# Two-layer encoder trunk on one core: a fourth unnormalised unit, keys and values in 512-column products, and other places for weight roundings and copies in ScalarE's and VectorE's queues

## The chip, the core and the metric

One NeuronCore of a Trainium2 chip runs the whole program. The metric is the device time of one execution in microseconds (us); lower is better. Beside the runs there is one execution recorded by the hardware profiler.

## What is computed

256 tokens of 1024 features go through two layers. Each layer is a mixer of three branches, a gated feed-forward network and a per-layer input gate:

```
h = rmsnorm(x);  q, k, v, cglu, sc_b, sc_c, sc_h, gates = split(h @ w_in)
y_a = window_attention(q, k, v, sinks, bias) @ w_attn_out     # 16 heads, 4 key/value heads of 64
c   = ca * sigmoid(cb)                       # cglu = [ca, cb], 1024 channels each
y_b = silu(layernorm(causal_dwconv31(c) + b)) @ w_conv_out
y_c = (sc_b * causal_dwconv3(sc_c * sc_h)) @ w_sc_out
x  += (g0*y_a + g1*y_b + g2*y_c) @ w_mix_out                  # g = sigmoid(gates)
x  += (silu(h2 @ w_gate) * (h2 @ w_up)) @ w_down              # h2 = rmsnorm(x), hidden 2816
x  += (p @ w_ple) * sigmoid(rmsnorm(x) @ w_ple_gate)
```

After both layers a final rmsnorm follows. All inputs are float32.

## The kernel before, in words

**Products in three parts.** Every product with a weight is made of three matmuls: high part of the weight by high part of the activation, high by low, low by high. The high part is a rounding to fp32r (ScalarE), the low part the rest (VectorE).

**The weight stream.** All weights come in one order, cut into chunks of sixteen 128x128 blocks (1 MB). SyncE loads chunk n into slot n % 5 of `w_raw` once the chunk five places ahead has been used. ScalarE rounds it to `w_hi` (`round_chunk`, L648, its copy is recorded as L646), VectorE subtracts it into `w_lo` (`low_chunk`, L1022 to L1027, recorded as L1026), and counts `lo_ready`. TensorE waits for `lo_ready` at the first block of each chunk. `after_chunk(c)` on either engine means: convert chunk c + 4 now. Nothing decides at run time: each engine carries out its own list in the order of the code, and the place of `after_chunk` between other steps is the place of that conversion in its queue.

**Strips.** A strip (`strip`, L359) is one 128-column piece of an output, with features on partitions and 256 tokens as moving columns: 8 blocks of contraction by 3 matmuls (L355 to L357). Strip s goes to bank s % 4 of PSUM, and waits until the strip four before it has been read (`bank_read`). Two strips use one chunk. In the later stages `tok_group` (L377, matmuls L393 to L395) works the other way round: tokens on partitions, 512 weight columns as moving ones, two chunks per group of 4 x 12 matmuls.

**Start of a layer.** The first stage (cglu) has 16 strips: 2u is the gate of unit u, 2u + 1 its value. The normalised h isn't ready when it begins. So the strips of units 0 to UNITS - 1 (3 units, strips 0 to 5) are computed from x times the gain (`u_src`), and VectorE multiplies with 1/rms afterwards: `raw_gate` (L1090, recorded L1093) reads the gate strip, ScalarE takes the sigmoid in place (`raw_activate`, L736, counts `gate_done`), and `raw_product` (L1096) waits for it, multiplies again (L1099) and multiplies the value strip into `cv` (L1103). From strip 6 on TensorE uses `h_hi`, `h_lo`: VectorE makes a tile of h (`normalise_tiles`, L1053), ScalarE rounds it (`round_h`, L669), VectorE subtracts (L1030). For later units ScalarE reads the bank itself (`activate`, L709) and VectorE makes one product (L1125).

In the same stretch ScalarE makes products for the 31-tap convolution of four channel tiles (`conv_products`, four at a time in this stage, L646 into `cprod`), which GpSimd adds up (L1511); a ring of four buffers and `pool_step` hold them together. VectorE carries out the taps of two other tiles (L1143, L1148), five per chunk.

**Queries, keys, values.** Twelve strips follow: two of K, two of V, eight of Q. ScalarE copies each out. Then TensorE turns V (four transposes, L468), ScalarE copies it to `v_tok`, and the attention runs inside the sc stage: step j holds weigh_values(j-2) (L503), scores(j) (L479, L481), a strip, and a second strip with `probs_transpose(j-1)` (L492) after its third block. `probs_transpose(t)` waits for `attn_lo` of head pair t - 1, which VectorE makes behind softmax(t + 1). ScalarE does, per step, exponentials(j) and then `copy_probs(j - 1)`.

**End of a layer.** The ple stage has eight short strips (two blocks each), which ScalarE copies out of their banks into `qm`; before the first it rounds a chunk. The ple_gate stage has eight strips of 8 blocks; x is updated tile by tile behind them, and the next layer's strip 0 needs all eight tiles.

## Time and profile before

| | us |
|---|---|
| runs of the kernel before | 1129.14, 1131.5, 1130.98 (median 1130.98) |
| profiled execution | 1129.25 |
| its span, first to last instruction | 1127.4 |
| TensorE busy | 1106.0 (98% of the span) |
| VectorE busy | 814.3 (72%) |
| ScalarE busy | 682.1 (61%) |
| GpSimd busy | 350.0 (31%) |
| mean granted TensorE clock | 0.995 of full speed |

The time of an execution has 1.8 us outside the span. Shares are means over the whole; the matmuls of TensorE overlap each other in the records, so a record's duration is longer than the time from its start to the next one's. In the timeline rows, the first number is the start in us from the span's start, the second the duration.

### The profile page before, as it was taken

The numbers are of one execution on the slowest core, as the hardware profiler recorded it, in microseconds if no ns is written. First come the engines' busy times: TensorE is split into PE (matmuls) and PEld (weight loads), VectorE is DVE, ScalarE is ACT, GpSimd is POOL, SyncE is SP. The second block draws the span as 40 slices with busy tenths as digits, with TensorE's granted clock in tenths as the row PEclk, the third lists the DMA queues.
The fourth block names the chain that finished last, engine by engine and source line by source line (L and its number), as shares of the span: only waits on it lengthen the run. The fifth ranks groups of instructions, "written<-read, shape, count | busy, mean of one in ns | idle before, by whom it ended". The sixth has DMA issues, their size and how long they took to land.

```text
span 1127.4 us, 18108 instructions
## 1 busy us (share of the span) xinstructions
PE 1106.0 (98%) x7202; PEld 1002.1 (89%) x7202; DVE 814.3 (72%) x1209; ACT 682.1 (61%) x1049; POOL 350.0 (31%) x319
## 2 busy tenths in 40 slices
PE   8899999999999999999989999999999999999997
PEld 8899899888898889889989989988888988998997
DVE  7987997898766554555799789878977665545554
ACT  6767875755746443445676788766475554334464
POOL 0787335874001000001129753458530100000011
PEclk9999999999999999999999999999999999999999
DMA  9564334555555545555545534355555455555541
GB/s 362 197 237 156 120 144 168 201 192 187 196 187 181 185 157 200 184 189 177 186 150 176 180 133 151 120 191 203 197 196 187 176 178 187 177 186 183 185 150 38
DMA packets 29347, 201.42 MB, mean 179 GB/s; under 512 B 3520, under 2 KB 3712, under 8 KB 5840
## 3 DMA queue, kind: packets, MB, share of 16 engines
q1 hardware_dynamic: 27648, 195.38, 49.4%
q0 software_dynamic: 1088, 4.74, 1.2%
q8 instruction: 57, 0.93, 0.3%
q10 hardware_dynamic: 528, 0.15, 0.1%
q14 instruction: 26, 0.21, 0.0%
HBM read 199.19 MB, written 3.69 MB: 180 GB/s over the span
## 4 chain that ended last, share of the span: by engine, by line
PE 90%; DVE 4%; ACT 3%; issue 1%; DMA 1%; SPq 0%; DVEq 0%
PE bank L393 15%; PE bank L395 15%; PE bank L394 15%; PE bank L355 14%; PE bank L356 14%; PE bank L357 14%; ACT w_hi L646 1%; DMA w_raw<-in_wstream 1%; DVE w_lo L1026 1%; PE bank L503 1%; PE bank L571 1%; PE bank L492 1%; PE bank L479 0%; PE bank L535 0%; ACT probs L772 0%
## 5 line engine op out<-in xcount | busy, mean ns | idle before, releaser
L1026 DVE TENSOR_TENSOR w_lo<-w_raw,w_hi 128x2048 fp32r<-128x2048 f32 x183 | 427.8, 2342 | 169.9 <-ACT w_hi L646 169.8
L646 ACT ACTIVATE w_hi<-w_raw 128x2048 fp32r<-128x2048 f32 (+1 forms) x185 | 350.7, 1899 | 116.3 <-DMA w_raw<-in_wstream 116.3
L1511 POOL TENSOR_TENSOR pacc<-pacc,cprod 128x256 f32<-128x256 f32 x224 | 253.1, 1130 | 124.8 <-ACT cprod L646 98.7
L355 PE MATMUL bank<-h_hi,w_hi 128*128 128x256 f32 x864 | 249.3, 289 | 6.1 <-issue 6.1
L356 PE MATMUL bank<-h_lo,w_hi 128*128 128x256 f32 x864 | 245.6, 284 | 0.0
L357 PE MATMUL bank<-h_hi,w_lo 128*128 128x256 f32 x864 | 245.5, 284 | 0.0
L393 PE MATMUL bank<-w_hi,h_hi 128*128 128x512 f32 x544 | 214.3, 394 | 0.0
L395 PE MATMUL bank<-w_hi,h_lo 128*128 128x512 f32 x544 | 212.1, 390 | 0.0
L394 PE MATMUL bank<-w_lo,h_hi 128*128 128x512 f32 x544 | 211.8, 389 | 0.0
L355 PE MATMUL bank<-act_hi,w_hi 128*128 128x256 f32 x608 | 173.8, 286 | 4.0 <-ACT qm L646 1.1
L355 PEld LDWEIGHTS bank<-h_hi,w_hi 128*128 128x128 f32 x864 | 166.8, 193 | 10.7 <-issue 10.7
L356 PE MATMUL bank<-act_lo,w_hi 128*128 128x256 f32 x608 | 172.0, 283 | 0.0
L357 PE MATMUL bank<-act_hi,w_lo 128*128 128x256 f32 x608 | 172.0, 283 | 0.0
L356 PEld LDWEIGHTS bank<-h_lo,w_hi 128*128 128x128 f32 x864 | 167.0, 193 | 0.0
L357 PEld LDWEIGHTS bank<-h_hi,w_lo 128*128 128x128 f32 x864 | 166.8, 193 | 0.0
L1474 POOL TENSOR_TENSOR sqsum<-cprod 128x256 f32<-128x256 f32 x6 | 4.4, 738 | 466.8 <-ACT cprod L662 466.8
L646 ACT ACTIVATE cprod<-cv,prms 128x256 f32<-128x256 f32 x248 | 113.0, 504 | 48.6 <-POOL pacc L1511 48.6
L355 PEld LDWEIGHTS bank<-act_hi,w_hi 128*128 128x128 f32 x608 | 116.5, 192 | 6.4 <-issue 1.9
L395 PEld LDWEIGHTS bank<-w_hi,h_lo 128*128 128x128 f32 x544 | 102.1, 188 | 21.8
L394 PEld LDWEIGHTS bank<-w_lo,h_hi 128*128 128x128 f32 x544 | 102.2, 188 | 20.5
L393 PEld LDWEIGHTS bank<-w_hi,h_hi 128*128 128x128 f32 x544 | 102.2, 188 | 20.4
L356 PEld LDWEIGHTS bank<-act_lo,w_hi 128*128 128x128 f32 x608 | 116.6, 192 | 0.3
(168 smaller groups left out, 1377.0 us busy)
## 6 DMA issues: line engine op xcount, KB each, us to landing
w_raw<-in_wstream SPq DMA_DIRECT2D x183, 1024.0 KB, 4.9
rel_bias_rows<-rel_bias_by_distance POOLq DMA_DIRECT2D x1, 2560.0 KB, 15.5
bias<-rel_bias_rows POOLq DMA_DIRECT2D x1, 1536.0 KB, 8.6
xs<-in_x SPq DMA_DIRECT2D x2, 512.0 KB, 5.6
w_raw<-in_wstream SPq DMA_DIRECT2D x2, 512.0 KB, 6.5
out_y<-xs SPq DMA_DIRECT2D x4, 256.0 KB, 2.4
zacc<-in_p POOLq DMA_DIRECT2D x2, 256.0 KB, 2.9
prms<-in_prm SPq DMA_DIRECT2D x1, 328.0 KB, 9.8
```

The source lines that it names most:

```text
L355: nc.tensor.matmul(o, wh, hi, start=first, stop=False, skip_group_check=True)
L356: nc.tensor.matmul(o, wh, lo, start=False, stop=False, skip_group_check=True)
L357: return nc.tensor.matmul(o, wl, hi, start=False, stop=last, skip_group_check=True)
L393: nc.tensor.matmul(o, hi[:, t0 + kt, rows], wh, start=kt == 0, stop=False, skip_group_check=True)
L394: nc.tensor.matmul(o, hi[:, t0 + kt, rows], wl, start=False, stop=False, skip_group_check=True)
L395: mm = nc.tensor.matmul(o, lo[:, t0 + kt, rows], wh, start=False, stop=kt == DT - 1, skip_group_check=True)
L492: mm = nc.tensor.transpose(psum[6 + e][:, c * P:(c + 1) * P], probs[:, t % 2, e, c * P:(c + 1) * P], idt[:, :])
L503: mm = nc.tensor.matmul(psum[6][rows, b * P:SEQ], v_tok[:, b, v], probs_t[:, e, b * SEQ:SEQ + b * P], start=b == 0, stop=b == 1, skip_grou ...
L571: mm = nc.tensor.transpose(psum[6 + n % 2][:, e * SEQ + b * P:e * SEQ + (b + 1) * P], prod[:, b, e * P:(e + 1) * P], idt[:, :])
L646: return nc.scalar.activation(o, i, ACT.Identity, **kw)
L1026: nc.vector.tensor_tensor(w_lo[:, slot, :], w_raw[:, slot, :], f32(w_hi[:, slot, :]), ALU.subtract).then_inc(lo_ready, 1)
L1511: nc.gpsimd.tensor_tensor(o, a, cprod[:, n % PROD_RING, :], ALU.add).then_inc(pool_step, 1)
```

## The change

It has five parts. (1) UNITS goes from 3 to 4, so strips 6 and 7 too use x times gain; the order of units, normalised tiles and the conversion of chunk 3 in both queues is another. (2) K and V are one `tok_group` of two chunks, tokens on partitions, columns 0 to 255 K and 256 to 511 V; now K is turned by four transposes, inside the second Q strip, and V is copied out directly. (3) In the sc stage ScalarE does `copy_probs(0)` before exponentials(1). (4) At the ple stage the conversion of one chunk goes behind the fourth strip's copy on ScalarE. (5) At the ple_gate stage ScalarE's rounding of the next layer's chunk 1 goes behind all eight tiles.

```diff
-UNITS = 3
+UNITS = 4
...
-                for s in range(2 * KT + QT):
-                    strip(L, S0["qkv"] + s, BPC * C0["qkv"] + DT * s, h_src, DT)
-
-
-                def v_transpose():
+                def turn_k():
+
                     for b in range(TB):
+                        pe.wait_ge(bank_read[2 + b], L * USES + S0["qkv"] // BANKS + 2)
+                        pe.wait_ge(bank_read[b], L * USES + S0["qkv"] // BANKS + 2)
                         for t in range(KT):
-                            if b == 0:
-                                wait_read(pe, L, S0["qkv"] + KT + t, (S0["qkv"] + KT + t) % BANKS)
-                            mm = nc.tensor.transpose(psum[6][:, b * KT * P + t * P:b * KT * P + (t + 1) * P],
-                                                     vv[:, t, b * P:(b + 1) * P], idt[:, :])
-                    mm.then_inc(vt_done, 1)
+                            mm = nc.tensor.transpose(psum[6][:, t * SEQ + b * P:t * SEQ + (b + 1) * P],
+                                                     k_tok[:, b, t * P:(t + 1) * P], idt[:, :])
+                    mm.then_inc(kt_done, 1)
+
+                tok_group(L, S0["qkv"], C0["qkv"], h_src, 0, L * USES + S0["qkv"] // BANKS + 1)
+                for s in range(2 * KT, 2 * KT + QT):
+                    strip(L, S0["qkv"] + s, BPC * C0["qkv"] + DT * s, h_src, DT, amid=turn_k if s == 2 * KT + 1 else None)
...
-                v_transpose()
+                pe.wait_ge(kk_ready, L + 1)
...
-                round_h(L * 3)
+                raw_activate(1, 2, ACT.Sigmoid)
                 round_chunk(L, AHEAD - 1)
+                round_h(L * 3, range(0, DT // 2))
+                raw_activate(2, 4, ACT.Sigmoid)
+                round_h(L * 3, range(DT // 2, DT))
                 for t in range(DT):
                     if t >= UNITS:
                         activate(t, 2 * t, ACT.Sigmoid, 2 * (t - 2) + 1)
-                    elif t > 0:
+                    elif t > 2:
                         raw_activate(t, 2 * t, ACT.Sigmoid)
...
+                def kv_out():
+
+                    s, use = S0["qkv"], L * USES + S0["qkv"] // BANKS + 1
+                    for b in range(TB):
+                        wait_strip(act, L, s + 2 + b)
+                        act.wait_ge(bank_read[2 + b], use)
+                        copy(k_tok[:, b, :], psum[b][:, 0:KT * P]).then_inc(bank_read[2 + b], 1)
+                        copy(v_tok[:, b, :], psum[b][:, KT * P:2 * KT * P]).then_inc(bank_read[b], 1)
+
+                def k_out():
+
+                    act.wait_ge(kt_done, L + 1)
+                    copy(kk[:, :, :].rearrange("p a b -> p (a b)"), psum[6][:, :]).then_inc(kk_ready, 1)
+
                 for s in range(2 * KT + QT):
-                    g = S0["qkv"] + s
-                    wait_strip(act, L, g)
-                    dst = kk[:, s, :] if s < KT else vv[:, s - KT, :] if s < 2 * KT else qm[:, s - 2 * KT, :]
-                    copy(dst, psum[g % BANKS][:, 0:SEQ], scale=1.0 if s < 2 * KT else HEAD_DIM ** -0.5
-                         ).then_inc(bank_read[g % BANKS], 1)
+                    if s == 2 * KT - 1:
+                        kv_out()
+                    if s >= 2 * KT:
+                        g = S0["qkv"] + s
+                        wait_strip(act, L, g)
+                        copy(qm[:, s - 2 * KT, :], psum[g % BANKS][:, 0:SEQ], scale=HEAD_DIM ** -0.5
+                             ).then_inc(bank_read[g % BANKS], 1)
+                    if s == 2 * KT + 2:
+                        k_out()
                     if s % 2:
                         after_chunk(C0["qkv"] + s // 2 - 1)
                         conv_products(before_qkv + QKV_PRODUCTS * (s // 2 + 1))
                 nc.scalar.activation(unused[:, :], eps[:, :], ACT.Exp)
-                act.wait_ge(vt_done, L + 1)
-                copy(v_tok[:, :, :], psum[6][:, 0:TB * KT * P].rearrange("p (b f) -> p b f", b=TB)).then_inc(vtok_ready, 1)
...
                     if j == 0:
                         exponentials(0)
                     after_chunk(C0["sc"] + j - 1)
+                    if j == 1:
+                        copy_probs(0)
                     if 0 < j < QT:
                         exponentials(j)
-                    if 0 <= j - 1 < QT:
+                    if 1 <= j - 1 < QT:
                         copy_probs(j - 1)
...
-                for c in range(done, DT * FB // BPC - 1):
-                    after_chunk(C0["down_b"] + c)
                 for t in range(DT):
                     s = S0["ple"] + t
                     wait_strip(act, L, s)
                     copy(qm[:, t, :], psum[s % BANKS][:, 0:SEQ]).then_inc(bank_read[s % BANKS], 1)
+                    if t == 3:
+                        for c in range(done, DT * FB // BPC - 1):
+                            after_chunk(C0["down_b"] + c)
...
-                    if t == 5:
-                        after_chunk(C0["ple_gate"] + 1)
 
                 for t in (DT - 2, DT - 1):
                     act.wait_ge(ple_added, L * DT + t + 1)
                     next_high(t)
                     square(L * 3 + 3, t)
-                after_chunk(C0["ple_gate"] + 2)
+                for c in (1, 2):
+                    after_chunk(C0["ple_gate"] + c)
...
+                def raw_unit(u):
+                    raw_gate(u, 2 * u)
+                    raw_product(cv[:, u, CPAD:], u, 2 * u + 1, u)
+
                 inverse(L * 3)
-                raw_gate(0, 0)
+                raw_unit(0)
+                raw_unit(1)
+                low_chunk(L, AHEAD - 1)
                 normalise_tiles(L * 3, L, G_MIX, range(0, DT // 2))
-                raw_product(cv[:, 0, CPAD:], 0, 1, 0)
+                raw_unit(2)
                 normalise_tiles(L * 3, L, G_MIX, range(DT // 2, DT))
-                raw_gate(1, 2)
-                low_chunk(L, AHEAD - 1)
-                raw_product(cv[:, 1, CPAD:], 1, 3, 1)
-                raw_gate(2, 4)
-                raw_product(cv[:, 2, CPAD:], 2, 5, 2)
+                raw_unit(3)
...
-        strips += [cols(k, t) for t in range(KT)] + [cols(v, t) for t in range(KT)]
+        strips.append(np.concatenate([side(m, 0, KT).reshape(DT, KT, P, P) for m in (k, v)], axis=1))
```

ScalarE's queue at the start of the first layer, before (`w_hi<-w_raw` are chunks 3, 4, 5; the sigmoids, L736, are those of units 0, 1 and 2, `cprod` the convolution products):

```order
L736 ACTIVATE gated<-gated 128x256 [waits bank_read0]
L646 ACTIVATE h_hi<-hf 128x256 [waits hf_ready] x8
L646 ACTIVATE w_hi<-w_raw 128x2048 [waits raw_loaded3]
L736 ACTIVATE gated<-gated 128x256 [waits bank_read2]
L646 ACTIVATE w_hi<-w_raw 128x2048 [waits raw_loaded4]
L646 ACTIVATE cprod<-cv,prms 128x256 [waits bank_read1]
L646 ACTIVATE cprod<-cv,prms 128x256 x3
L736 ACTIVATE gated<-gated 128x256 [waits bank_read0]
L646 ACTIVATE w_hi<-w_raw 128x2048 [waits raw_loaded0]
```

The same place in the changed kernel (line numbers are its own; L734 are the sigmoids of units 0 to 3):

```order
L734 ACTIVATE gated<-gated 128x256 [waits bank_read0]
L734 ACTIVATE gated<-gated 128x256 [waits bank_read2]
L644 ACTIVATE w_hi<-w_raw 128x2048 [waits raw_loaded3]
L644 ACTIVATE h_hi<-hf 128x256 [waits hf_ready] x4
L734 ACTIVATE gated<-gated 128x256 [waits bank_read0]
L644 ACTIVATE h_hi<-hf 128x256 [waits hf_ready] x4
L644 ACTIVATE w_hi<-w_raw 128x2048 [waits raw_loaded4]
L644 ACTIVATE cprod<-cv,prms 128x256 [waits bank_read1]
L644 ACTIVATE cprod<-cv,prms 128x256 x3
L644 ACTIVATE w_hi<-w_raw 128x2048 [waits raw_loaded0]
L644 ACTIVATE cprod<-cv,prms 128x256 [waits pool_step] x4
L734 ACTIVATE gated<-gated 128x256 [waits bank_read2]
```

Units 0 and 1 and chunk 3 moved ahead of the normalised tiles; the last row is the sigmoid of unit 3, behind chunks 4 and 5 and eight products.

VectorE's queue at the end of the normalised tiles, in the changed kernel (L1111, L1117, L1121 are unit 3, the first `w_lo` row is chunk 4, the next chunk 5):

```order
L1048 TENSOR_TENSOR h_lo<-hf,h_hi 128x256 [waits hhi_ready] x2
L1111 TENSOR_TENSOR gated<-bank,rstd 128x256 [waits strip_done]
L1117 TENSOR_TENSOR gated<-gated,rstd 128x256 [waits gate_done]
L1121 TENSOR_TENSOR cv<-bank,gated 128x256 [waits strip_done,gate_scaled]
L1044 TENSOR_TENSOR w_lo<-w_raw,w_hi 128x2048 [waits hi_ready]
L1163 TENSOR_SCALAR bank<-cv,prms 128x256 [waits bank_read3]
L1168 SCALAR_TENSOR_TENSOR bank<-cv,prms,bank 128x256 [waits conv_step] x4
L1044 TENSOR_TENSOR w_lo<-w_raw,w_hi 128x2048 [waits hi_ready]
```

Before, three units (of them unit 0 amid the tiles) and chunk 3 stood ahead of chunk 4; now unit 3 is the last step ahead of it.

## Rows read from the trace of the kernel before

**Rows 1.** Waits of TensorE: line, waited for, us in total, times, longest.
```profile
PE bank L355 <- issue: 6.1, 2, 3.7
PE bank L503 <- ACT probs_t L646: 3.3, 2, 1.7
...
PE bank L355 <- ACT qm L646: 1.1, 2, 0.6
```

**Rows 2.** Timeline of TensorE around strips 6 to 8, first layer: start, duration.
```profile
29.00 0.28 PE L357 MATMUL bank<-act_hi,w_lo 128*128 128x256 f32 x1
32.97 0.50 PE L355 MATMUL bank<-h_hi,w_hi 128*128 128x256 f32 x1 [3.69 <-issue]
...
37.42 0.28 PE L355 MATMUL bank<-h_hi,w_hi 128*128 128x256 f32 x1
...
40.30 0.28 PE L355 MATMUL bank<-h_hi,w_hi 128*128 128x256 f32 x1
```

**Rows 3.** Stretch table: us, busy of PE, PEld, DVE, ACT, POOL; clock, DMA.
```profile
32.97:36.38 3.41, 3.41 (x16) 3.41 (x17) 2.66 (x6) 3.41 (x7) 2.19 (x3) 0.51 0.56 232
```

**Rows 4.** Timeline of VectorE, start of the first layer.
```profile
21.73 0.42 DVE L1093 TENSOR_TENSOR gated<-bank,rstd 128x256 f32<-128x256 f32 x1
22.07 0.87 DVE L1053 SCALAR_TENSOR_TENSOR hf<-xs,prms,rstd 128x256 f32<-128x256 f32 x2
...
24.49 0.42 DVE L1099 TENSOR_TENSOR gated<-gated,rstd 128x256 f32<-128x256 f32 x1
24.95 0.42 DVE L1103 TENSOR_TENSOR cv<-bank,gated 128x256 f32<-128x256 f32 x1
...
30.58 2.29 DVE L1026 TENSOR_TENSOR w_lo<-w_raw,w_hi 128x2048 fp32r<-128x2048 f32 x1 [1.04 <-ACT w_hi L646]
...
35.97 2.37 DVE L1026 TENSOR_TENSOR w_lo<-w_raw,w_hi 128x2048 fp32r<-128x2048 f32 x1
```

**Rows 5.** Timeline of ScalarE in the same stretch.
```profile
22.18 0.42 ACT L736 ACTIVATE gated<-gated 128x256 f32<-128x256 f32 x1 [2.82 <-DVE gated L1093]
...
28.65 1.90 ACT L646 ACTIVATE w_hi<-w_raw 128x2048 fp32r<-128x2048 f32 x1
...
30.76 1.89 ACT L646 ACTIVATE w_hi<-w_raw 128x2048 fp32r<-128x2048 f32 x1
32.56 1.78 ACT L646 ACTIVATE cprod<-cv,prms 128x256 f32<-128x256 f32 x4
34.25 0.40 ACT L736 ACTIVATE gated<-gated 128x256 f32<-128x256 f32 x1
34.55 1.90 ACT L646 ACTIVATE w_hi<-w_raw 128x2048 fp32r<-128x2048 f32 x1
```

**Rows 6.** Timeline of VectorE, second layer's start.
```profile
568.27 5.04 DVE L1026 TENSOR_TENSOR w_lo<-w_raw,w_hi 128x2048 fp32r<-128x2048 f32 x2
...
575.01 0.42 DVE L1093 TENSOR_TENSOR gated<-bank,rstd 128x256 f32<-128x256 f32 x1
```

**Rows 7.** Timeline of TensorE, second layer: first matmuls of strips 6 and 8.
```profile
586.26 0.55 PE L355 MATMUL bank<-h_hi,w_hi 128*128 128x256 f32 x1 [2.42 <-issue]
...
593.46 0.28 PE L355 MATMUL bank<-h_hi,w_hi 128*128 128x256 f32 x1
```

**Rows 8.** Timeline of VectorE, later in the cglu stage.
```profile
50.70 2.30 DVE L1026 TENSOR_TENSOR w_lo<-w_raw,w_hi 128x2048 fp32r<-128x2048 f32 x1
52.92 2.04 DVE L1148 SCALAR_TENSOR_TENSOR bank<-cv,prms,bank 128x256 f32<-128x256 f32 x5
...
55.22 2.44 DVE L1026 TENSOR_TENSOR w_lo<-w_raw,w_hi 128x2048 fp32r<-128x2048 f32 x1
```

**Rows 9.** Timeline of TensorE in a stage with 512 moving columns.
```profile
200.03 0.39 PE L394 MATMUL bank<-w_lo,act_hi 128*128 128x512 f32 x1
200.26 0.39 PE L395 MATMUL bank<-w_hi,act_lo 128*128 128x512 f32 x1
200.48 0.39 PE L393 MATMUL bank<-w_hi,act_hi 128*128 128x512 f32 x1
```

**Rows 10.** Timeline of VectorE in step 2 of the sc stage.
```profile
119.55 0.41 DVE L1030 TENSOR_TENSOR act_lo<-bank,act_hi 128x256 fp32r<-128x256 f32 x1
```

**Rows 11.** Timeline of TensorE in the same step.
```profile
120.11 0.85 PE L492 MATMUL bank<-idt,probs 128*128 128x128 f32 x6 [0.16 <-DVE act_lo L1030]
```

More of the change, by code:

```diff
@@ L172, in build @@
         kk = sb("kk", [P, KT, SEQ])
-        vv = part
+        k_tok = part
         v_tok = sb("v_tok", [P, TB, KT * P])
@@ L239, in build @@
         hlo_ready = sem("hlo_ready")
-        vt_done = sem("vt_done")
-        vtok_ready = sem("vtok_ready")
+        kt_done = sem("kt_done")
+        kk_ready = sem("kk_ready")
         s_done = sem("s_done")
@@ L488, in probs_transpose @@
                             pe.wait_ge(attn_lo, L * QT + t)
-                        if e == 0 and t == 0:
-                            pe.wait_ge(vtok_ready, L + 1)
                         for c in range(3):
@@ L498, in weigh_values @@
                     pe.wait_ge(pt_copied, L * 2 * QT + 2 * t + 2)
-                    pe.wait_ge(vtok_ready, L + 1)
                     for b in range(TB):
@@ L667, in root, with round_h @@
                 nc.scalar.activation(rstd[:, :], psum[4][:, 0:SEQ], ACT.Sqrt, bias=eps[:, :]).then_inc(std_ready, 1)
-            def round_h(q):
-                for t in range(DT):
+            def round_h(q, tiles):
+                for t in tiles:
                     act.wait_ge(hf_ready, q // 3 * DT + t + 1)
```

## The prediction

> **What bounds the kernel now.** I read the page first: TensorE is busy in 98% of the span, so only two things can shorten the kernel, fewer TensorE cycles or fewer of its waits. Then the waits of TensorE [rows 1]. The reader is to see that they are few: two of 3.7 and 2.4 us put down to "issue", two before weigh_values (3.3 us in all), two of some 0.6 us on ScalarE's `qm` copies. Then the timelines around each, to see what really ended it. The first "issue" wait lies before strip 6: the matmul before it starts at 29.00 and strip 6 at 32.97 [rows 2]. It isn't h that is late but chunk 3: VectorE's subtraction runs from 30.58 to 32.87 [rows 4] and TensorE starts 0.10 later. Its rounding starts at 28.65 [rows 5], behind all eight tiles of h. The second layer repeats this. A stall costs more than its length: in the 3.4 us behind it the granted clock is 0.51, that is the lower level, 1.2 GHz [rows 3]. At full clock a strip takes 40.30 - 37.42 = 2.88 us [rows 2], so two take 5.76; strips 6 and 7 took 7.33 in the first layer [rows 2] and 7.20 in the second [rows 7], 1.57 and 1.44 us more.
>
> **Part 1, the fourth unit, layer 1.** I follow the changed queues with the durations of before; all times are on the clock of the old trace, where everything up to the first raw gate (21.73) stays. Unit 0: gate at 21.73, its sigmoid 0.45 later [rows 4, 5], the multiplication with 1/rms 0.45 after that (sigmoid 0.42, hand-over 0.03), the product 0.46 later (24.49 to 24.95), the next gate 0.34 later (21.73 to 22.07): 1.70 in all [rows 4]. Unit 1's gate is at 23.43, its sigmoid at 23.88, the rounding of chunk 3 0.30 later (34.25 to 34.55 [rows 5]) at 24.18. Rounding and subtraction took 28.65 to 32.87, 4.22 [rows 4, 5], so chunk 3 is ready at 28.40, ahead of strip 6 (29.12): the old stall goes, and strip 8 could start at 29.12 + 5.76 = 34.88.
>
> It can't, because of chunk 4. The first tile of h starts at about 28.35; four tiles later comes unit 2's gate, 2.42 after the first tile (22.07 to 24.49 [rows 4]), 30.77; its product 0.45 + 0.45 + 0.46 later, 32.13 (0.1 more for ScalarE's last tile in between: 32.2). From such a product to the next rounding, across the last four tiles, it took 24.95 to 28.65, 3.70 [rows 4, 5]: chunk 4's rounding starts at 35.9. ScalarE then has, **ahead of unit 3's sigmoid**, chunk 4 (1.80, from 30.76 to 32.56), four products (1.69, to 34.25), chunk 5 (1.80) and four more products (1.69): 6.98 [rows 5]. The sigmoid starts at 42.9. VectorE stands at unit 3 all this time, and chunk 4's subtraction stands behind unit 3 on VectorE. From sigmoid to the end of the subtraction it took 34.25 to 35.97 + 2.37 = 38.34, 4.09 [rows 4, 5]; with 0.10 to TensorE, strip 8 starts at 47.1 instead of 40.30: **+6.8**. TensorE idles some 12 us, and resumes on the lower clock: another 1.57, since the old loss lies within the old 40.30. Behind the wait on VectorE queue chunk 4's and 5's subtractions and the early taps; ScalarE isn't held. They catch up: a round of subtraction, five taps and a product takes 4.52 (50.70 to 55.22 [rows 8]) against 5.76 per chunk on TensorE, so I cost them at nothing; uncovered, each lost round would cost up to 5.8 - 4.5, with the sign against the kernel.
>
> **Layer 2.** The same chain is 25.4 long from the first raw gate (47.1 - 21.73). That gate was at 575.01, behind a pair of subtractions of 5.04 [rows 6]. Part 5 puts both roundings behind the last tile; the two then take 1.8 + 1.9 and the last subtraction 2.3 where the pair took 5.04: +1.0. The last tile itself comes sooner, since no 1.9 us rounding is ahead of it. Bounds of the net: 0 and 1.9; I take 0.5, nearer the small end. So strip 8 starts at 575.01 + 0.5 + 25.4 = 600.9 instead of 593.46 [rows 7]: **+7.4**, and the clock again, 1.44. Part 5's gain at strip 0 is swallowed here: strip 8 hangs on the queues, not on when strip 0 began.
>
> **Part 2, K and V.** Removed: 4 strips, 96 matmuls of 256 columns, one per 2.88 / 24 = 0.120 us, 11.52. Added: 48 of 512 columns, one per 0.227 (200.03 to 200.48 is two [rows 9]), 10.90. The recorded durations (0.28 and 0.39) would say 26.9 against 18.7, but they overlap. **-0.6 per layer, -1.2 in all.** Transposes and copies are as many as before; V's copy leaves the stretch before exponentials(0), K's goes between Q copies, hidden under strips of 2.88.
> The Trainium skill, page "TensorE: Matmul & The Clock Gate", section "Back-to-back issue gap", gives about 131 ns for a sustained 512-column matmul; by that the group would take 6.3 us and the change save 5.2 a layer, 9 us more in all than I count. The trace contradicts it for these fp32r products (0.227), and the trace decides.
>
> **Part 3, copy_probs(0).** TensorE's 1.65 us wait before weigh_values(0) goes, two times [rows 1]. What is late next: 14 matmuls and the scores later comes `probs_transpose(1)`, which waits for `attn_lo` of pair 0. VectorE reaches it at 119.55 to 119.96 [rows 10], and TensorE already waited there (it starts at 120.11 [rows 11]). VectorE's row of steps to it doesn't start at weigh_values, so TensorE merely waits 1.7 us later. Bounds: -3.3 (all kept) and +2.9 (nothing kept, and a wait of about 2 us that drops the clock as the 2.4 us one did). I take **0**, since the row shows the next wait in place.
>
> **Part 4, ple copies.** The 1.1 us before strip 4's bank go [rows 1]: the four copies are done before the rounding. The rounding ends before strip 4's own copy is needed by ple_gate. **-1.1**; bounds -1.5 and 0.
>
> **Sum.** 6.8 + 1.6 + 7.4 + 1.4 - 1.2 + 0 - 1.1 = +14.9. From the profiled execution's own 1129.25 that is 1144.1. The median of the runs before lies 1.7 above that execution, which I can't carry over in full, since three runs spread by 2.4; I take 0.7 of it: **1144.8**.
>
> **Rivals.**
> A, the other side: *nothing takes the old stall's place.* It needs chunk 4 at TensorE by 34.9, 12 us earlier than above, so either unit 3's sigmoid isn't awaited by VectorE's next subtraction, or ScalarE reaches it before chunk 4. For it: the old stall does go (chunk 3 is ready 0.7 early). Against: the order of both queues. It decides from the point where the subtraction ends before 40.2; between that and 34.9 the change is faster. Time: -6.1 of waits [rows 1], -3.0 of clock, -1.2, -1.1 (and up to -3.3 for part 3): 1129.25 - 11.4 = 1117.9, down to 1114.6. Chance 0.06.
> The same page of the Trainium skill (section "Architectural detail: the array is 16× 32×32, not 1× 128×128") says that ScalarE's and VectorE's queues are strictly first in, first out. By that rule the subtraction of chunk 4 can't pass unit 3, and A is out; rows 4 and 5 show no step that passed another.
> B: *as forecast, but with a tail.* The late convolution products, VectorE's catch-up, or a clock fall in the attention stage add to it: +3 for a clock fall in both layers, up to 1.3 for each of some rounds not caught up. For: TensorE's new wait in part 3 (about 2 us) lies between waits of 1.65 without and 2.4 with a fall. Time: 1147 to 1151. Chance 0.17.
> C: *the sigmoid comes sooner than I count*, because ScalarE's products overlap or unit 3's steps take 0.42 where the old ones were stretched. Each layer up to 1.5 less, and part 3 kept: 1138 to 1141. Chance 0.10.
> D: *the change isn't what it says*, unit 3 is still normalised in time by another path, or the parts cancel. Then within 0.2% of before, 1128.7 to 1133.2. Chance 0.02.
>
> **How the numbers follow.** The forecast has 0.65; the time is its own. The range takes in most of B and C: 1139.5 to 1149.5, which leaves out A, D and the far ends of B and C, some 0.15. A measurement of this kernel tells from no change about 0.2%, 2.3 us. Slower by more: forecast, B and C, 0.92. Same: D, 0.02. Faster: A, 0.06.
>
> **What would show it.** In the changed trace: no wait before strip 6 in either layer; one of about 12 us before strip 8, put down to "issue" or VectorE's `w_lo`, with the clock near 0.5 in the 3.4 us behind it; VectorE idle for 6 to 7 us before the second multiplication of unit 3; ScalarE's fourth in-place sigmoid behind two roundings and eight products. 48 matmuls of 512 columns 0.227 apart in 10.9 us. No wait before weigh_values(0), but one of 1.5 to 2 us before `probs_transpose(1)`. No `qm` wait at the ple stage. I am wrong if strip 8 follows strip 7 without a gap, if the 512-column pitch of that group is much below 0.227, or if the clock stays low long after the stall.

## The result, and the profile after

| | before | changed |
|---|---|---|
| median of 4 runs | 1130.17 (1129.14 to 1131.5) | 1144.32 (1143.9 to 1145.2) |
| profiled execution, its span | 1129.25, 1127.4 | 1143.97, 1141.8 |

The ratio is 1.0123, 95% interval 1.0111 to 1.0135: 14 us slower, against 1144.8 forecast. The page's part 1 of the changed kernel has nearly the same busy times on every engine as before, in a longer span (the 96 matmuls fewer are the K/V groups):

```profile
PE 1104.6 (97%) x7106; PEld 997.7 (87%) x7106; DVE 813.8 (71%) x1213; ACT 682.3 (60%) x1049; POOL 350.2 (31%) x319
```

TensorE's waits in the changed kernel (line, waited for, us in total, times, longest):

```profile
PE bank L355 <- issue: 22.6, 2, 11.7
PE bank L491 <- DVE act_lo L1048: 3.7, 2, 1.9
```

The "issue" waits have grown from 6.1 to 22.6 [rows 1]. Those before weigh_values and at the ple stage are gone from the list, and one before `probs_transpose(1)` is new. The timeline of TensorE shows that the large ones lie before strip 8 of each layer:

```profile
34.52 0.28 PE L357 MATMUL bank<-act_hi,w_lo 128*128 128x256 f32 x1
46.46 0.55 PE L355 MATMUL bank<-h_hi,w_hi 128*128 128x256 f32 x1 [11.66 <-issue]
...
607.22 0.55 PE L355 MATMUL bank<-h_hi,w_hi 128*128 128x256 f32 x1 [10.95 <-issue]
```

Strips 6 and 7 now follow strip 5 without a gap, where strip 6 had waited [rows 2]. The "gaps" below are from the start of the last matmul before a wait to the start of the next one: 11.94 and 11.23 us here. Matmuls that don't wait start 0.12 us apart, so that much of a gap is no wait. "Issue" names nobody, so the next step is ScalarE's timeline in the gap:

```profile
35.56 0.42 ACT L644 ACTIVATE h_hi<-hf 128x256 fp32r<-128x256 f32 x1 [0.32 <-DVE hf L1071]
35.88 1.89 ACT L644 ACTIVATE w_hi<-w_raw 128x2048 fp32r<-128x2048 f32 x1
37.68 1.78 ACT L644 ACTIVATE cprod<-cv,prms 128x256 f32<-128x256 f32 x4
39.37 1.89 ACT L644 ACTIVATE w_hi<-w_raw 128x2048 fp32r<-128x2048 f32 x1
41.17 1.69 ACT L644 ACTIVATE cprod<-cv,prms 128x256 f32<-128x256 f32 x4
42.76 0.40 ACT L734 ACTIVATE gated<-gated 128x256 f32<-128x256 f32 x1
```

and VectorE's:

```profile
36.35 0.42 DVE L1111 TENSOR_TENSOR gated<-bank,rstd 128x256 f32<-128x256 f32 x1
43.19 0.42 DVE L1117 TENSOR_TENSOR gated<-gated,rstd 128x256 f32<-128x256 f32 x1 [6.43 <-ACT gated L734]
43.65 0.42 DVE L1121 TENSOR_TENSOR cv<-bank,gated 128x256 f32<-128x256 f32 x1
43.99 2.36 DVE L1044 TENSOR_TENSOR w_lo<-w_raw,w_hi 128x2048 fp32r<-128x2048 f32 x1
```

Read together: chunk 4 is rounded by 37.8, but its low part starts at 43.99, because VectorE stands for 6.43 us at unit 3, whose sigmoid comes after two roundings and eight convolution products. TensorE starts 0.11 after the subtraction ends. The stretch table (us, busy of PE, PEld, DVE, ACT, POOL; granted clock, DMA) shows the price behind the gap:

```profile
46.46:51.20 4.74, 4.74 (x22) 4.74 (x23) 4.60 (x7) 0.51 (x1) 4.31 (x4) 0.50 0.00 2
...
607.22:611.50 4.28, 4.28 (x20) 4.28 (x21) 4.14 (x6) 0.51 (x1) 3.85 (x4) 0.50 0.00 0
```

The granted clock is 0.50 there, the lower level, 1.2 GHz. It stays so until 52.02 in the first layer and 611.81 in the second, 5.6 and 4.6 us of matmuls, where it was 3.4 before [rows 3].

The new wait in the attention and K/V's group, on TensorE and VectorE:

```profile
125.98 0.28 PE L357 MATMUL bank<-h_hi,w_lo 128*128 128x256 f32 x1
128.12 0.41 PE L491 MATMUL bank<-idt,probs 128*128 128x128 f32 x2 [1.87 <-DVE act_lo L1048]
```

```profile
127.56 0.42 DVE L1048 TENSOR_TENSOR act_lo<-bank,act_hi 128x256 fp32r<-128x256 f32 x1
```

```profile
72.00 0.40 PE L393 MATMUL bank<-w_hi,h_hi 128*128 128x512 f32 x1
...
82.91 0.28 PE L355 MATMUL bank<-h_hi,w_hi 128*128 128x256 f32 x1
```

A ledger of how late the changed kernel is at one place after another, each against the same place in the kernel before: strip 10 of layer 1 +8.66 (54.72 against 46.06), scores(0) +8.02, probs_transpose(1) +8.0 (128.12 against 120.11, [rows 11]), ple's mean square +7.2, strip 10 of layer 2 +15.84 (615.06 against 599.22), scores(0) +15.2, last instruction +14.4. So 8.66 comes in at each layer's start, 0.64 goes at each K/V group and 0.8 at each ple stage, and nothing changes in the attention.

### The profile page after: what moved, and what is told of

The parts are those of the page before. It is cut to its first block, busy times and chain, and to the rows that moved or that the text cites. A ratio compares the mean times of both kernels' runs of the same rounds, so it can differ in the third digit from the quotient of the medians.

```text
span 1141.8 us, 17902 instructions
## 1 busy us (share of the span) xinstructions
PE 1104.6 (97%) x7106; PEld 997.7 (87%) x7106; DVE 813.8 (71%) x1213; ACT 682.3 (60%) x1049; POOL 350.2 (31%) x319
## 4 chain that ended last, share of the span: by engine, by line
PE 92%; DVE 3%; issue 2%; ACT 2%; DMA 0%; DVEq 0%
PE bank L393 15%; PE bank L395 15%; PE bank L394 15%; PE bank L355 14%; PE bank L356 14%; PE bank L357 14%; PE bank L501 1%; DVE w_lo L1044 1%; PE bank L569 1%; PE bank L491 1%; ACT w_hi L644 1%; DMA gain<-in_gain 0%; PE bank L480 0%; PE bank L533 0%; ACT act_hi L644 0%
## 5 line engine op out<-in xcount | busy, mean ns | idle before, releaser
L355 PE MATMUL bank<-h_hi,w_hi 128*128 128x256 f32 x768 | 223.0, 290 | 22.6 <-issue 22.6
L393 PE MATMUL bank<-w_hi,h_hi 128*128 128x512 f32 x576 | 226.7, 394 | 0.0
L395 PE MATMUL bank<-w_hi,h_lo 128*128 128x512 f32 x576 | 224.5, 390 | 0.0
L394 PE MATMUL bank<-w_lo,h_hi 128*128 128x512 f32 x576 | 224.3, 389 | 0.0
L356 PE MATMUL bank<-h_lo,w_hi 128*128 128x256 f32 x768 | 219.1, 285 | 0.0
L357 PE MATMUL bank<-h_hi,w_lo 128*128 128x256 f32 x768 | 218.9, 285 | 0.0
L356 PE MATMUL bank<-act_lo,w_hi 128*128 128x256 f32 x640 | 181.0, 283 | 0.0
L355 PEld LDWEIGHTS bank<-h_hi,w_hi 128*128 128x128 f32 x768 | 149.1, 194 | 27.3 <-issue 27.2
L356 PEld LDWEIGHTS bank<-h_lo,w_hi 128*128 128x128 f32 x768 | 149.3, 194 | 0.1
L357 PEld LDWEIGHTS bank<-h_hi,w_lo 128*128 128x128 f32 x768 | 149.1, 194 | 0.0
```

Of the source, the lines that this page charges most:

```text
L355: nc.tensor.matmul(o, wh, hi, start=first, stop=False, skip_group_check=True)
L356: nc.tensor.matmul(o, wh, lo, start=False, stop=False, skip_group_check=True)
L357: return nc.tensor.matmul(o, wl, hi, start=False, stop=last, skip_group_check=True)
L393: nc.tensor.matmul(o, hi[:, t0 + kt, rows], wh, start=kt == 0, stop=False, skip_group_check=True)
L394: nc.tensor.matmul(o, hi[:, t0 + kt, rows], wl, start=False, stop=False, skip_group_check=True)
L395: mm = nc.tensor.matmul(o, lo[:, t0 + kt, rows], wh, start=False, stop=kt == DT - 1, skip_group_check=True)
```

## Experiments

**1. Unit 3's sigmoid alone, moved.** On ScalarE only, against the changed kernel:

```diff
                 round_h(L * 3, range(DT // 2, DT))
+                raw_activate(3, 6, ACT.Sigmoid)
                 for t in range(DT):
...
-                    elif t > 2:
-                        raw_activate(t, 2 * t, ACT.Sigmoid)
```

> The changed kernel with one move: ScalarE takes unit 3's sigmoid right behind the last tile of h, ahead of chunk 4's rounding, the eight products and chunk 5's. Queue theory (chunk 4's subtraction waits behind unit 3, which waits for ScalarE): VectorE's gate of unit 3 ends at 36.8, the sigmoid follows, chunk 4 is rounded 37.1 to 39.0 and subtracted by 41.4, so strip 8 starts at 41.4 instead of 46.5, in the second layer also about 5 earlier; less clock loss as well: 1134 us, 10 less than the changed kernel, 4 more than the kernel before. Rival 1 (chunk 4 is late because its own rounding or its load is late, unit 3 only stands beside it): strip 8 still at 46.5, 1144. Rival 2 (fourth unit's extra VectorE work costs the time): no change either, within 1 us of 1144.

Measured 1136.5, ratio 1.0052 (1.0037 to 1.0067). Strip 8 starts at 41.43 instead of 46.46, and what ends its wait is now chunk 4's rounding, which stands behind the eighth tile of h:

```profile
36.79 0.42 ACT L734 ACTIVATE gated<-gated 128x256 f32<-128x256 f32 x1 [0.83 <-DVE gated L1110]
37.11 1.89 ACT L644 ACTIVATE w_hi<-w_raw 128x2048 fp32r<-128x2048 f32 x1
39.04 2.29 DVE L1043 TENSOR_TENSOR w_lo<-w_raw,w_hi 128x2048 fp32r<-128x2048 f32 x1 [0.92 <-ACT w_hi L644]
41.43 0.55 PE L355 MATMUL bank<-h_hi,w_hi 128*128 128x256 f32 x1 [6.39 <-issue]
```

TensorE's waits:

```profile
PE bank L355 <- issue: 12.3, 2, 6.4
PE bank L491 <- DVE act_lo L1047: 3.7, 2, 1.9
PE bank L355 <- ACT v_tok L644: 2.3, 2, 1.5
```

One instruction's place in ScalarE's queue is worth 8 of the 14 us. The gaps before strip 8 are still 6.67 and 6.21. 1134 was expected. The third row has 2.3 us of what is missing: with the start 5 us earlier ScalarE is held by GpSimd's ring of four products, and V's copy comes late. In the recorded execution a fall of the clock in the attention took another 1.5 (the last section has its row).

**2. Part 1 alone.** The kernel before with the four units and the order of both queues around them, nothing else:

```diff
-UNITS = 3
+UNITS = 4
...
-                round_h(L * 3)
+                raw_activate(1, 2, ACT.Sigmoid)
                 round_chunk(L, AHEAD - 1)
+                round_h(L * 3, range(0, DT // 2))
+                raw_activate(2, 4, ACT.Sigmoid)
+                round_h(L * 3, range(DT // 2, DT))
...
```

> The kernel before with part 1 alone (fourth unit, new order at a layer's start); K and V as four strips, the copies and roundings elsewhere as before. Queue theory: part 1 is worth +16.5 (8.7 in the first layer; in the second 7.2 to 8.7, since part 5's later roundings are missing), so 1146 to 1147, slower than the changed kernel by 2 to 3. Rival (the loss comes from the K/V group or from an interplay of parts): 1135 or less.

Measured 1146.03, ratio 1.0144 (1.0125 to 1.0164). Its profile has gaps of 11.93 and 10.41 before strip 8. All of the slowdown is part 1's: 8 us of it the place of unit 3's sigmoid, by experiment 1.

**3. All but part 1.** The changed kernel with part 1 undone, so with parts 2 to 5:

```diff
-UNITS = 4
+UNITS = 3
```

> The changed kernel with part 1 undone: three units in the old order, parts 2 to 5 as changed. Queue theory: -1.2 for K and V, -1.4 for the ple stage, 0 for copy_probs, and up to -0.5 at the second layer's start: 1127.3, with both old waits of 3.9 and 2.7 us before strip 6 back and the wait before probs_transpose(1) at about 2.1 us. Rival (part 3 does pay by itself when the layer's start doesn't disturb it): 1124.

Measured 1128.43 (10 runs), ratio 0.9979 (0.9967 to 0.9991). The start's stall is back before strip 6, with gaps of 4.22 and 3.55 where they had been 3.97 and 2.70. The 0.85 more in layer 2 isn't what part 5 costs. Counted from the mean square of the ple stage, strip 0 starts 0.38 sooner (28.17 instead of 28.55) and strip 6 0.31 later (47.38 instead of 47.07): the price is 0.3, and the rest of the longer gap is strips 0 to 5 being done sooner. After the shorter of the two gaps no fall of the clock followed in the recorded execution:

```profile
586.20:590.00 3.80, 3.80 (x34) 3.80 (x33) 3.08 (x5) 3.80 (x7) 2.38 (x4) 1.00 0.13 52
33.20:38.30 5.10, 5.10 (x25) 5.10 (x26) 4.35 (x6) 4.92 (x10) 3.49 (x4) 0.53 0.33 135
```

**4. Part 3 alone.** The kernel before, and on ScalarE:

```diff
+                    if j == 1:
+                        copy_probs(0)
                     if 0 < j < QT:
                         exponentials(j)
-                    if 0 <= j - 1 < QT:
+                    if 1 <= j - 1 < QT:
                         copy_probs(j - 1)
```

> The kernel before with part 3 alone: copy_probs(0) ahead of exponentials(1). Theory that the wait only moves: the 1.8 us before weigh_values(0) go in both layers, and the wait before probs_transpose(1) grows from 0.3 to 2.1: 1130.2, the same within 0.2%, perhaps 0.3 worse, since V's copy still stands ahead of exponentials(0). Rival (VectorE's chain starts from scores(2) and moves with TensorE): -3.3, 1126.9.

Measured 1130.47, ratio 0.9997 (0.9987 to 1.0007). The wait before weigh_values(0) goes and one before `probs_transpose(1)` comes (3.8 us in two, where the old had been 3.3): the same time.

**5. Part 2 alone.** The kernel before, and on TensorE (with its copies and the weights' order as in the change):

```diff
-                for s in range(2 * KT + QT):
+                tok_group(L, S0["qkv"], C0["qkv"], h_src, 0, L * USES + S0["qkv"] // BANKS + 1)
+                for s in range(2 * KT, 2 * KT + QT):
...
```

> The kernel before with part 2 alone: K and V as one group of 48 matmuls with 512 columns. Pitch theory (0.120 us per 256-column matmul, 0.227 per 512-column one, whatever the recorded durations say): -0.6 per layer, 1129.0 if 1130.2 is the kernel before, ratio 0.9989. V's copy also leaves ScalarE's way to exponentials(0), so the waits in the attention stage may shrink by up to 0.5 each. Rival (recorded durations 0.28 and 0.39 are the cost): -8 per layer, 1114.

Measured 1128.78 (11 runs; before 1130.92), ratio 0.9981 (0.9972 to 0.9989), 2.1 us less. The pitch (the time from one matmul's start to the next one's) accounts for 1.2, at the edge of the interval, and the recorded execution has just that: from strip 6 to scores(0) it is 0.70 shorter in the first layer and 0.51 in the second. Where the other 0.9 comes from isn't shown. Part of it may be the clock: of the 20 runs of the kernel before, 8 had a mean granted clock of 0.991, of these 11 none had less than 0.993.

**6. Chunks 3, 4 and 5 early.** On top of experiment 1, ScalarE rounds all three before the first tile of h, VectorE makes 3 and 4 before the tiles and 5 before unit 3:

```diff
-                round_chunk(L, AHEAD - 1)
+                for n in (3, 4, 5):
+                    round_chunk(L, n)
                 round_h(L * 3, range(0, DT // 2))
...
-                        after_chunk(t - 1)
+                        if t > 2:
+                            after_chunk(t - 1)
...
```

> The kernel of e1 with chunks 4 and 5 rounded right behind chunk 3 on ScalarE, chunk 4 subtracted right behind chunk 3 and chunk 5 ahead of unit 3 on VectorE. Queue theory: chunk 4 is ready at 30.7, four us ahead of strip 8 (34.7); strip 8 loses at most 1.6 us to the last tiles of h (tile 7 at 38.7 where 37.2 is wanted), and the clock doesn't fall. But the convolution products start at 38.9 against strip 8 at 34.7, so GpSimd's ring holds ScalarE: I expect a wait for ScalarE before strip 12 (1 to 3 us) and before the first Q strip (3 to 7 us). Together 1122 to 1127, still 10 under e1. Rival (the late data of chunk 4 isn't the last thing, h is): strip 8 starts after 38.

Measured 1135.49, ratio 1.0038 (1.0025 to 1.0052), 8 us or more above what was expected. The wait before strip 8 is gone, another stands before strip 12:

```profile
PE bank L355 <- ACT gated L707: 7.2, 2, 3.7
PE bank L491 <- DVE act_lo L1049: 3.7, 2, 1.9
```

ScalarE's timeline shows why: it stands at the products, and strip 8's gate is read only then.

```profile
47.49 1.29 ACT L644 ACTIVATE cprod<-cv,prms 128x256 f32<-128x256 f32 x3
50.67 0.51 ACT L644 ACTIVATE cprod<-cv,prms 128x256 f32<-128x256 f32 x1 [1.89 <-POOL pacc L1534]
51.09 0.36 ACT L707 ACTIVATE gated<-bank 128x256 f32<-128x256 f32 x1
```

**7. The same with fewer products in this stage**, none at the first step of K and V, and the late ones over more chunks:

```diff
-CGLU_PRODUCTS, QKV_PRODUCTS, SC_PRODUCTS = 4, 4, 3
-LATE_CHUNKS = 8
+CGLU_PRODUCTS, QKV_PRODUCTS, SC_PRODUCTS = 3, 4, 3
+LATE_CHUNKS = 10
...
```

> The kernel of e6 with the convolution products spread otherwise: three instead of four per chunk in the cglu stage, none at the first step of the qkv stage, the rest in ten instead of eight later steps. If GpSimd's ring is what holds ScalarE in e6, its waits before strip 12 and before the Q strips go or fall under 1 us and nothing is late at the conv mean: 1118 to 1120. Rival (ScalarE's own work, not the ring, is late): as e6, or slower where the products come later.

Measured 1135.26, ratio 1.0036 (1.0022 to 1.005), again far above what was expected. TensorE's waits for ScalarE's gates and copies went, and two others came in each layer: gaps of 2.5 and 2.7 before strip 12, for a low part that VectorE makes behind ten taps, and one of 3.56 at the convolution's mean. Ten chunks are too many: in experiment 12, with nine, the second is gone.

```profile
PE bank L545 <- POOL sqsum L1547: 6.3, 2, 3.2
```

**8. Attention: the low part first.** Experiment 3 with the low part of attn(j - 2) ahead of softmax(j) on VectorE:

```diff
+                    if 0 <= j - 2 < QT:
+                        low_attn(j - 2)
                     if j < QT:
                         softmax(j)
...
-                    if 0 <= j - 2 < QT:
-                        low_attn(j - 2)
```

> The kernel of e3 (parts 2 to 5 without part 1) with VectorE's subtraction for attn_lo ahead of softmax instead of behind it. If the wait before probs_transpose(1) is VectorE's order alone, it falls from 2.1 to about 0.6 us in both layers, -3.0 together: ratio 0.995 to before, 3 us under e3. Rival (that wait hangs on scale_probs(1) or on ScalarE's rounding): within 1 us of e3.

Measured 1127.08, ratio 0.9964 (0.9955 to 0.9974), the lowest median here, though its interval overlaps those of experiments 3 and 11. It is 1.35 less than experiment 3, and not the 3 that were expected. Of the gap of 2.15 some 0.7 is left, and a new one of 1.6 per layer stands before weigh_values(1):

```profile
PE bank L501 <- ACT probs_t L644: 2.7, 2, 1.3
```

**9. Early chunks, spread out.** As 7, but chunks 6 to 11 one step earlier on both engines, and other numbers of products. On VectorE:

```diff
-                    if t > 2:
-                        after_chunk(t - 1)
-                    taps(min(CGLU_TAPS * t, CGLU_DONE) if t < DT - 1 else CGLU_DONE)
+                    if 1 < t < 5:
+                        after_chunk(t)
+                    if t > 0:
+                        taps(min(CGLU_TAPS * t, CGLU_DONE) if t < DT - 1 else CGLU_DONE)
+                    if t > 4:
+                        after_chunk(t)
```

> The change with unit 3's sigmoid first, chunks 3, 4 and 5 rounded in a row before the first tiles, and now every later cglu chunk (6 to 11) one step earlier on both engines instead of from the third step on, so that VectorE no longer makes ten taps ahead of chunk 6's low part; GpSimd's products 3 a step in the cglu part, none at the first qkv step, 5 at the others, and the rest over nine chunks instead of ten. The run before this one had lost the start's stall but had got waits of 2.5 and 2.7 us before strip 12 and of 3.6 us at the convolution's mean, each in both layers, and 3.4 us of half clock behind each. Theory (those were places where work that had been put off fell due, and no new law): all four go, 1135.3 - 5.1 - 7.1 - some 4 of clock = 1119, 1117 to 1122. Rival (ScalarE and VectorE are full between strips 8 and 16, so whatever is moved from before strip 8 comes back as a wait there or in the qkv part): a wait of 2 us or more of TensorE for a chunk's low part, ScalarE's copies or the gates, and 1127 to 1136.

Measured 1136.51, ratio 1.005 (1.0035 to 1.0065). The rival was nearer: TensorE still waits for the gates, and the longest wait is now in the attention, which neither had named. The expectation also counted the lower clock behind the waits before strip 12. In experiment 7's profile it had followed only those at the mean (0.58 from 266.50 to 270.00); behind strip 12 the clock was 1.00 (50.35 to 54.00, 606.22 to 610.00).

```profile
PE bank L491 <- DVE act_lo L1051: 5.7, 2, 2.8
PE bank L355 <- ACT gated L707: 3.6, 2, 2.0
PE bank L501 <- ACT probs_t L644: 3.1, 2, 1.6
```

**10. The same with both moves in the attention**, that of 8 and on ScalarE:

```diff
-                    if j == 1:
-                        copy_probs(0)
+                    if j in (1, 2):
+                        copy_probs(j - 1)
...
-                    if 1 <= j - 1 < QT:
+                    if 2 <= j - 1 < QT:
```

> The kernel of the run before plus the attention's order: the low part of attn(t-2) ahead of softmax(t) on VectorE, and copy_probs(1) ahead of exponentials(2) on ScalarE as copy_probs(0) is. Theory (the two waits of 2.15 us before the values of block 2 go, the one of 1.6 before weigh_values(1) that took their place does not come): 3 to 4 us less than that run, plus what a clock fall behind them had cost. Rival (with copy_probs(1) first, the exponentials of 2 come late and transposing them waits instead): the same as that run within 1 us.

Measured 1135.3, ratio 1.0037 (1.0023 to 1.0052): 1.2 less in the median, not 3 to 4, and the intervals overlap. The recorded executions took the same, 1135.39 here and 1135.34 in experiment 9, so this is the rival's outcome. TensorE's waits for `probs_t` are now eight, 6.8 us, those for `act_lo` 2.8: 9.6 together, where they had been 3.1 and 5.7, 8.8 together.

**11. Experiment 3 with both moves in the attention.**

> The change without part 1, with both moves in the attention. The run with the low part alone ahead had 1127.08 and waits of 1.62 us before weigh_values(1) in each layer, from copy_probs(1) behind exponentials(2). Theory: with copy_probs(1) ahead those go to the 0.5 us or so of a step's own chain, 1.1 us less a layer: 1124.9, ratio 0.9945. Rival: exponentials(2), late by copy_probs(1)'s 1 us, let transpose(2) or its values wait by as much, and the time stays at 1127.

Measured 1127.37, ratio 0.9971 (0.9959 to 0.9983), the same as experiment 8. The two waits of 1.3 became six:

```profile
PE bank L355 <- issue: 7.4, 2, 4.1
PE bank L501 <- ACT probs_t L644: 2.8, 6, 0.6
```

**12. Experiment 7 with two edits**, the low part first as in 8 and:

```diff
-LATE_CHUNKS = 10
+LATE_CHUNKS = 9
```

> The kernel that had chunks 3 to 5 rounded early and three products a step (1135.26), with two edits: its late products spread over nine chunks instead of ten, and the low part of attn(t-2) ahead of softmax(t) on VectorE. In its profile the wait of 3.56 us at the convolution's mean stood in each layer with 3.4 us of half clock behind it, and the values of block 2 waited 1.8 and 2.1 us. Theory (each of these waits is its own and nothing but PE's time stands behind it): 7.1 and some 3.4 of clock go at the mean, 2 to 3 in the attention, so 1122, ratio 0.992, the fastest of all. Rival (VectorE and ScalarE are full and each wait removed comes back in the next place, as it did in the three kernels with early chunks so far): 1130 or more, with a new wait of over 2 us named in the profile.

Measured 1128.46 (1125.59 to 1132.55, 10 runs), ratio 0.9985 (0.9971 to 1.0). The waits at the mean went and nothing took their place: 6.8 less than experiment 7. That is about half of what was expected, and neither theory's number. In the attention the waits for `act_lo` fell from 3.4 to 0.4 and one of 2.7 for `probs_t` came. What is left:

```profile
PE bank L355 <- DVE w_lo L1045: 5.6, 3, 2.4
PE bank L501 <- ACT probs_t L644: 2.7, 2, 1.3
```

So four units, with everything around them put in order, come to the time of three (experiment 3), and not below it. The fair comparison is experiment 8, which has three units and the same order in the attention: 0.9964 (0.9955 to 0.9974) against 0.9985 (0.9971 to 1.0), so the fourth unit gained nothing and may have cost 1 or 2 us. A reason why no more is to be had may lie in VectorE's share of the stretch from the first raw gate to 60 us, in the kernel before, in experiment 3, the changed kernel and this one (one row of the stretch table each: us, busy of PE, PEld, DVE, ACT, POOL; clock, DMA):

```profile
22.00:60.00 38.00, 34.31 (x274) 34.14 (x273) 35.66 (x61) 27.56 (x44) 23.39 (x19) 0.96 0.68 242
```

```profile
22.00:60.00 38.00, 34.06 (x266) 33.89 (x265) 35.66 (x61) 27.78 (x44) 23.31 (x19) 0.91 0.66 233
```

```profile
22.00:60.00 38.00, 26.34 (x200) 26.17 (x198) 28.55 (x49) 22.96 (x37) 17.10 (x16) 0.82 0.49 182
```

```profile
22.00:60.00 38.00, 35.37 (x284) 34.17 (x283) 34.45 (x59) 25.57 (x40) 15.18 (x13) 1.00 0.65 233
```

VectorE was busy for 35.66 of 38 us (94%) in the kernel before, TensorE for 34.31: both are nearly full. VectorE's raw units, tiles, low parts and taps must all be done there, and an order mostly chooses which of TensorE's waits they make. The changed kernel lost 7 us of VectorE there (28.55). Kernel 12 starts the K/V group at 62.1, experiment 3 at 64.1, the changed kernel at 72.0: the start did gain 2 us on three units. In the recorded executions the second layer gave most of them back, with a gap of 2.67 and the lower clock for 3.3 us behind it, where experiment 3's gap of 3.55 had cost no clock. That VectorE's load is the limit is argued from these rows and not shown. Against it speaks that a round of VectorE takes 4.52 and a chunk on TensorE 5.76 [rows 8], so that VectorE is short of time only in the first part of this stretch; a kernel with less work on VectorE there wasn't tried.

## Why the prediction was right

- *Part 1, layer 1, +6.8 and 1.57 for the clock.* The order of events came out as followed through the queues: chunk 3 ready at 28.46 (forecast 28.40), chunk 4's rounding at 35.88 (35.9), the sigmoid at 42.76 (42.9), strip 8 at 46.46 (47.1). Most of the 0.64 lies between sigmoid and TensorE: 3.70 instead of 4.19. In the old chain from which the 4.09 came, the multiplication by 1/rms is recorded with 0.91 us (at 34.68), in the new one with 0.42; why the old one was longer isn't shown. Against that the clock took more: strips 8 and 9 last from 46.46 to 54.72, 8.26 where 5.76 is full clock, 2.5 and not 1.57. That 6.16 + 2.50 = 8.66 measured comes so near to the 8.4 forecast is in part luck, since the two misses cancel. The step that was mis-sized is the clock's term, for which I had carried over the loss behind a stall of a third of the length. Experiment 2 shows that the loss is part 1's, and experiment 1 that 8 us of it hang on the place of unit 3's sigmoid. With that moved, a gap of 6.67 is left behind chunk 4's rounding.
- *Layer 2, +7.4 and 1.44.* The first raw gate is 0.32 later than the shift of 7.19 carries it (575.01 [rows 6] to 582.52; 0.5 forecast), the chain behind it 24.70 (25.4), the clock 2.1 (607.22 to 615.06 for two strips) instead of 1.44. 8.84 forecast, 8.65 measured, again with two misses that cancel.
- *Part 2, -0.6 per layer.* 72.00 to 82.91 is 10.91, forecast 10.90; the ledger has -0.64. The 0.227 per 512-column product held against the Trainium skill's 131 ns (page "TensorE: Matmul & The Clock Gate", section "Back-to-back issue gap"), by which, as an estimate, the group would have taken 6.3. Alone the part measured 2.1 in all, of which 0.9 isn't in the recorded execution.
- *Part 3, 0.* The wait moved to `probs_transpose(1)`, 1.87 of idle time instead of 1.65 plus 0.16; ledger and experiment 4 both say 0. The prediction placed `probs_transpose(1)` 14 matmuls and the scores behind weigh_values(0). The trace of before has 33 matmuls of strips there beside the scores. Nothing in the sum hung on it. The rival of a clock fall behind it didn't happen in the changed kernel; in experiment 1's profile it did, in layer 1.
- *Part 4, -1.1.* The ledger has -0.8 in each of the two layers, -1.6. [rows 1] give these waits as 0.6 each, but the gap from matmul to matmul was 0.84 in either layer, and all of it went.
- *Part 5, +0.5 within layer 2's term.* It cost 0.3, in the changed kernel and in experiment 3.
- *The sum.* Starts 17.3 (17.2 forecast), K/V -1.3 (-1.2), attention 0, ple -1.6 (-1.1): 14.4 in the spans, where 14.9 was forecast. The starts came out so near only because in each the chain was counted too long and the clock's loss too small.
- *Rivals.* A (nothing takes the stall's place) was out by the order of the queues. Experiments 6, 7, 9 and 10 show more: even with that order mended, the next wait stood in line. B's tail didn't come: the changed kernel is as late at the convolution's mean (273.11 against 265.09) as at scores(0), 8.02. Of C the shorter chain came, 24.70 instead of 25.4 in either layer, but part 3's gain wasn't kept.

## What to carry to other kernels

When a static order moves one step, follow both queues as far as the first instruction that waits for the other engine, and ask what stands ahead of the partner: here one 0.4 us sigmoid behind 7 us of other work cost 8 us over the two layers, in a change that did remove the wait it was made for. Before reordering to remove a wait, read each engine's share in that stretch alone: VectorE's share of 72% over the whole hid one of 94% at the start, and of the kernels that moved work there or in the attention most only moved the wait.

## What the runs showed of the hardware that was not expected

How much clock a stall costs isn't read from its length. Gaps of 11.94 and 11.23 were followed by the lower level for 5.6 and 4.6 us of matmuls, one of 4.22 by 5.1 us at 0.53. The gap of 3.55 before strip 6 of layer 2 cost no clock in experiment 3 (1.00 from 586.20 to 590.00), and a gap of the same length at the same place did in experiment 8 (0.50 from 586.35 to 590.00). The gap of 2.66 before strip 12 of layer 2 cost none in experiment 7 (1.00 from 606.22 to 610.00). In experiment 12 one of 2.67 there was followed by this stretch, which begins 1.2 us after TensorE had resumed:

```profile
602.40:605.70 3.30, 3.30 (x18) 3.30 (x17) 3.30 (x5) 2.69 (x4) 3.01 (x3) 0.50 0.19 77
```

And in experiment 1's profile the wait of 2.15 us in the attention, which in the changed kernel cost no clock, was followed by the lower level in layer 1:

```profile
124.60:127.80 3.20, 3.20 (x18) 2.98 (x18) 3.13 (x6) 2.81 (x10) 1.27 (x2) 0.50 0.03 8
```

Such falls make part of the spread of a kernel's runs. Of the 20 runs of the kernel before beside experiment 5, those with a mean granted clock of 0.994 or 0.995 took 1129.18 to 1130.72, those at 0.991 1131.10 to 1131.94. The spread of 7 us in experiment 12 isn't explained by it: runs of 1126.15 and 1129.55 both had 0.996. Its cause stays open.
